# Index weights folded into the key's projection, packed sample index scores, paired value products, and projection steps placed between top-k and rotations

## The chip, the cores and the metric

The kernel runs on one core of a Trainium2 chip. The metric is the device time of one execution in microseconds (us). The kernel before took 1411.16 us, the median of three runs (1410.94 to 1413.31).

## The reference, cut to what matters

One layer of a hybrid model runs on a prompt of 512 tokens and on 8 sample sequences of 4 new tokens each (32 sample tokens), so every projection has 544 columns. The part that the change touches is the sparse attention (branch A):

```python
p = rmsnorm(x, norm_mix_g) @ w_in        # -> a_q, a_k, a_v, i_q, i_k, i_w, p_b, c_q, gates
i_q, i_k = rope_partial(...), rope_partial(...)      # 4 index heads of 64, one index key
i_w = i_w * ((4 * 64) ** -0.5)                       # one weight per token and index head
s = relu(einsum('bqhd,bld->bqhl', iq, ik))
score = einsum('bqhl,bqh->bql', s, iw)               # causal, then top-k
# prompt: 512 keys, top 128; sample: 1024 cached keys + 4 new, top 256
s = einsum(q, k_sel) * 64 ** -0.5; p = softmax(s); o = einsum(p, v_sel)   # 8 heads, 2 kv heads
```

Then follow the RWKV branch, cross attention, a gated merge, an MLP and the final norm. They are untouched.

## The kernel before, in words

Every engine has its own program, written out by hand, and semaphores order them. The projections are a list of jobs (`JOBS`). A job multiplies 8 blocks of 128 contraction rows (`KT` = 8) with the normalised input in two halves of 272 columns, 16 matmuls, all fp32; the profile has two records for each fp32 matmul. Its weights come in slabs of up to 1 MB through a ring of five (`RING`), sent by SyncE's queue (SP), which waits with a slab until the jobs of the slab five before it are done.

The stages around the change, in the order of time:

1. **First jobs.** TensorE runs four jobs (`job`, L811): `ik` (the index key, written twice, to partitions 0 to 63 and 64 to 127, by loading its weights twice), `iw` (the four index weights, 4 columns wide), and two `iq`. ScalarE evacuates each (L1453). Then three rotary rotations follow (`rope`: TensorE L864, VectorE L1782 and L1785, GpSimd L692), TensorE transposes the index weights (L884), and VectorE scales them (L1807, L1808) and copies them to the partitions of the sample's rows (L1810).
2. **Prompt top-k.** TensorE computes the prompt's index scores (L893), then the other six jobs (`aq`, `ak`, `av`). VectorE combines heads and finds the top 128 of each of three blocks of tokens with 16 rounds of `take_eight` (L1822, L1823). While it does, TensorE computes the sample's index scores (L904, L906): for each of 8 sequences a `zi` tile of 128 columns that is zero but for 16 of them, accumulated in the same banks 4 to 6.
3. **Sample scores and rotations.** VectorE applies relu and weight (L1844), TensorE sums heads with a 0/1 matrix `sel` (L911), VectorE copies the sums to `ss` (L1846, L1847). Five more rotations follow, then the transposes of the values (L921) and their copy on ScalarE (L1511, L1512).
4. **Units.** 32 units, one for each of 4 token blocks t and 8 heads (`NU` = 32; u // 8 is t). In iteration u TensorE issues the score of unit u (`p_score`, L936 and, for the mask, L938), the transposes of unit u-2 (`p_turn`, L947), the value product of unit u-3 (`p_out`, L956, output on 64 partitions) and then fill steps. VectorE in iteration u takes the maximum of unit u (L1867, L1868), normalises unit u-1 (L1873, L1874), and does one `take_eight` of the sample's top-k on `ss`. ScalarE takes the exponential (L1520) and copies the transposes (L1529). The widths grow with t: 128(t+1) keys.
5. **Sample attention** on gathered cache rows (`kvb`, from L993), then cross attention, RWKV and the rest.

**Fill steps.** `fill_plan` hands out the matmuls of later jobs (mk, mv, cq, pb, gate) one contraction block at a time to tags in TensorE's program: `fill(tag)` issues as many steps as the tag's budget says. A step is one matmul of 256 or 272 columns (L836, L839, L841). The tags ("p", u) have 5 steps each; in this stage the plan may not go past job pb 13, which leaves 160 steps (64 for mk and mv, 64 for cq, 32 for pb 12 and 13). The 160 are used up at u = 31. ScalarE evacuates a job with `evacs(tag)` where its last step was filled.

SP's queue sends, one after the other: the first slabs, 64 index-key pages (`ki`, L543), slabs 5 to 12, then the kv pages (8 groups of 8) and slabs 13 to 16.

```python
waits = [(("p", u), 5) for u in range(35)] + ...
...
for u in range(NU + 3):
    if u < NU: p_score(u)
    if 2 <= u < NU + 2: p_turn(u - 2)
    if u >= 3: p_out(u - 3)
    fill("p", u)
```

Of the kernel before, what the change touches and what calls it, by code (L numbers as in the profile page):

```python
# [27 lines left out]
P = 128  # L28
# [19 lines left out]
RING = 5  # L48
# [17 lines left out]
def constants():  # L66
# [34 lines left out]
    c["sel"][r, r % 32] = 1.0  # L101
# [30 lines left out]
def slab_plan():  # L132
# [4 lines left out]
    s = [("w_in", 0, KT, [(IK, 64), (IK, 64), (IK + 64, 4)]), ("w_in", 0, KT, [(IQ, 256)])]  # L137
# [17 lines left out]
def job_plan():  # L155


    jobs = [("ik", 0, 0, 0, 128, "a"), ("iw", 0, 0, 128, 4, "a"), ("iq", 0, 1, 0, 128, "a"), ("iq", 1, 1, 128, 128, "a")]
# [75 lines left out]
def fill_plan():  # L234
# [3 lines left out]
    waits = [(("p", u), 5) for u in range(35)] + [(("need", "cq", 3), 0), (("need", "pb", 13), 0), (("close", "p", 0), 0)]  # L238
# [42 lines left out]
KV_SLAB = slabs_before(("p",), ("need", "cq", 3), ("need", "pb", 13), ("close", "p", 0)) + RING  # L281
# [27 lines left out]
def build(nc, i, o):  # L309
    with ExitStack() as ctx:  # L310
# [84 lines left out]
        zi = R[:, B + 2048:B + 3200]  # L395
# [30 lines left out]
        iwc, iws = small[:, 0:20], small[:, 20:21]  # L426
# [364 lines left out]
        def _(pe):  # L791
# [82 lines left out]
            for n in range(4):  # L874
                job(n, xn3)
# [5 lines left out]
            out_of(1, pe)  # L881
            for t in range(5):
                w = P if t < 4 else NS
                mm = pe.transpose(ps[0:w, 7, 4 * t:4 * t + 4], iwT[0:4, P * t:P * t + w], ident[0:4, 0:4])  # L884
            mm.then_inc(s["iw_tok"], 1)

            pe.wait_ge(s["zi_set"], 5)
# [7 lines left out]
            for n in range(4, FILL0):  # L895
                job(n, xn3)

            pe.wait_ge(s["zi_set"], 4)
# [3 lines left out]
            for b in range(DB):  # L902
                for h in range(2):
                    pe.matmul(ps[:, 4 + h, :], zi[0:64, P * b:P * (b + 1)], ki[b][:, 512 * h:512 * (h + 1)],  # L904
                              start=(b == 0), stop=(b == DB - 1))
                pe.matmul(ps[:, 6, 0:NS], zi[0:64, P * b:P * (b + 1)], ik[0:64, SEQ:TOK],  # L906
                          start=(b == 0), stop=(b == DB - 1)).then_inc(s["ki_used"], 1)
            pe.wait_ge(s["rs"], 1)
            for h in range(3):
                w = 512 if h < 2 else NS  # L910
                mm = pe.matmul(ps[0:NS, 4 + h, 0:w], k_("sel"), rs[:, 512 * h:512 * h + w], start=True, stop=True)  # L911
            mm.then_inc(s["ssum"], 1)
            pe.wait_ge(s["ss_out"], 1)
            for n in range(3, 8):
                rope(n)

# [5 lines left out]
            mm.then_inc(s["v_tok"], 1)  # L922

# [8 lines left out]
            def p_score(u):  # L932
                t, ht, hp, half = unit(u)
                if u >= 3:
                    pe.wait_ge(s["p_exp"], u - 2)
# [14 lines left out]
            def p_out(u):  # L950
                t, ht, hp, half = unit(u)
                pe.wait_ge(s["p_pT_out"], u + 1)
                if u % 8 == 0 and t >= 1:
                    pe.wait_ge(s["oA_out"], t)
                for k in range(t + 1):
                    mm = pe.matmul(ps[hp, 0, P * ht:P * (ht + 1)], vt[:, k, hp], ppt[:, u % 2, k],  # L956
                                   start=(k == 0), stop=(k == t))
                mm.then_inc(s["pav_done"], 1)
# [6 lines left out]
            for u in range(NU + 3):  # L965
                if u < NU:
                    p_score(u)
                if 2 <= u < NU + 2:
                    p_turn(u - 2)
                if u == 1:  # L970
                    pe.wait_ge(s["ss_out"], 1)
                if u >= 3:
                    p_out(u - 3)
# [11 lines left out]
            quarter = [slice(32 * g, 32 * g + 32) for g in range(4)]  # L985
# [427 lines left out]
        def _(act):  # L1413
# [25 lines left out]
            def evac(n):  # L1439
# [3 lines left out]
                src = ps[0:min(w, P), b:b + 2, 0:HALF]  # L1443
                fn = ACT.Copy
# [5 lines left out]
                else:  # L1450
                    dst = {"ik": lambda: ik, "iw": lambda: iwT[0:4], "iq": lambda: iq[:, idx], "aq": lambda: aq3[:, idx],
# [48 lines left out]
            for n in range(4):  # L1500
                evac(n)
# [6 lines left out]
            for n in range(4, FILL0):  # L1508
                evac(n)
# [690 lines left out]
```

## Time and profile before

| | |
|---|---|
| median of three runs | 1411.16 us |
| the profiled execution's own time | 1411.86 us |
| its span (first to last instruction) | 1409.0 us |
| PE (TensorE matmul) busy | 1310.1 us, 93% |
| DVE (VectorE) busy | 667.4 us, 47% |
| ACT (ScalarE) busy | 370.9 us, 26% |
| chain that ended last | PE 85%, DVE 10%, ACT 2%, issue 2% |

Times are from the start of the span. A row's busy time is that of a group of instructions; a bracket behind a row is the idle time of that engine before it and what ended it. A PE record is about 0.2 us longer than the distance to the next one, because matmuls are pipelined: for a rate, subtract starts.

### The profile page before, as it was taken

To read this page: it belongs to the slowest core of one execution; us is meant where nothing else is said; L and a number is where in the kernel's file an instruction comes from. 1 tells how busy PE (TensorE), PEld (TensorE's weight loads), DVE (VectorE), ACT (ScalarE), POOL (GpSimd) and SP (SyncE) were. 2 spreads that over 40 slices of the span, in tenths; PEclk is the share of its full clock that TensorE was granted. 3 is DMA by queue.
4 is the path that set the end of the run, shared out by engine and by line. 5 is a ranking of instruction groups with operands and counts; after the bars stand their busy time and mean duration, and the time that the engine had idled before them with its cause. 6 is when DMAs were issued, how large, how long until landed. Compare 5 with 4: busy or idle time off the path is not lost.

```text
span 1409.0 us, 26535 instructions
## 1 busy us (share of the span) xinstructions
PE 1310.1 (93%) x11320; PEld 1107.2 (79%) x11324; DVE 667.4 (47%) x1119; ACT 370.9 (26%) x732; POOL 76.6 (5%) x150
## 2 busy tenths in 40 slices
PE   5898899989979999999989997989599999999995
PEld 4575566668667677688778677989599999999995
DVE  4299797744152452452343324743644334334235
ACT  3110122334323122223223222222333213223121
POOL 0100200002111021011001000000000000000000
PEclk9999899999989999999999999999899999999997
DMA  7122143404300101130220006542122222222201
GB/s 290 31 71 103 61 143 116 161 31 164 135 32 9 69 32 53 51 100 10 68 87 18 25 35 235 182 152 90 35 86 90 90 90 90 91 90 90 90 31 63
DMA packets 38646, 123.04 MB, mean 87 GB/s; under 512 B 5138, under 2 KB 17426, under 8 KB 29570
## 3 DMA queue, kind: packets, MB, share of 16 engines
q1 hardware_dynamic: 37090, 116.80, 23.6%
q0 software_dynamic: 1440, 4.56, 0.9%
q8 instruction: 89, 1.46, 0.4%
q14 instruction: 27, 0.22, 0.1%
HBM read 109.44 MB, written 11.90 MB: 86 GB/s over the span
## 4 chain that ended last, share of the span: by engine, by line
PE 85%; DVE 10%; ACT 2%; issue 2%; DMA 1%; SPq 0%; DVEq 0%; ACTq 0%
PE ps L841 23%; PE ps L1359 12%; PE ps L1360 12%; PE ps L1363 12%; PE ps L811 2%; PE ps L1110 2%; DVE R L1823 2%; DVE small L1822 2%; PE ps L936 2%; PE ps L956 2%; PE ps L836 1%; PE ps L839 1%; PE ps L1160 1%; PE ps L1196 1%; PE ps L1198 1%
## 5 line engine op out<-in xcount | busy, mean ns | idle before, releaser
L841 PE MATMUL ps<-xn,ring 128*128 128x272 f32 x1344 | 354.2, 407 | 0.9 <-ACT aq L1560 0.9
L841 PEld LDWEIGHTS ps<-xn,ring 128*128 128x128 f32 x1344 | 246.3, 192 | 61.8 <-issue 11.1
L524 DVE TENSOR_TENSOR wl<-land,wh 128x1024 fp32r<-128x1024 f32 (+1 forms) x96 | 104.7, 1092 | 193.8 <-ACT wh L516 193.0
L516 ACT ACTIVATE wh<-land 128x1024 fp32r<-128x1024 f32 (+1 forms) x96 | 91.2, 951 | 237.2 <-PE ps L1363 228.8
L1359 PE MATMUL ps<-xhi,wh 128*128 128x272 f32 x512 | 139.4, 290 | 9.0 <-DVE xlo L1775 6.8
L1360 PE MATMUL ps<-xlo,wh 128*128 128x272 f32 x512 | 139.1, 291 | 0.0
L1360 PE MATMUL ps<-hl,wh 128*128 128x272 f32 x512 | 138.2, 289 | 0.0
L1359 PE MATMUL ps<-hh,wh 128*128 128x272 f32 x512 | 138.1, 288 | 0.0
L1363 PE MATMUL ps<-xhi,wl 128*128 128x272 f32 x512 | 106.8, 290 | 0.0
L1363 PE MATMUL ps<-hh,wl 128*128 128x272 f32 x512 | 106.1, 288 | 0.0
L1359 PEld LDWEIGHTS ps<-xhi,wh 128*128 128x128 f32 x512 | 97.3, 190 | 9.9 <-issue 7.5
L1360 PEld LDWEIGHTS ps<-xlo,wh 128*128 128x128 f32 x512 | 97.4, 190 | 0.0
L1360 PEld LDWEIGHTS ps<-hl,wh 128*128 128x128 f32 x512 | 96.4, 188 | 0.0
L1359 PEld LDWEIGHTS ps<-hh,wh 128*128 128x128 f32 x512 | 96.3, 188 | 0.0
L811 PE MATMUL ps<-xn,ring 128*128 128x272 f32 (+1 forms) x320 | 76.1, 400 | 5.8 <-DVE xn L1757 3.5
L1363 PEld LDWEIGHTS ps<-xhi,wl 128*128 128x128 f32 x512 | 80.8, 190 | 0.0
L1363 PEld LDWEIGHTS ps<-hh,wl 128*128 128x128 f32 x512 | 80.1, 188 | 0.0
L811 PEld LDWEIGHTS ps<-xn,ring 128*128 128x128 f32 (+1 forms) x320 | 58.2, 183 | 24.0 <-issue 4.3
L2116 DVE TENSOR_TENSOR mlpt<-mlpt 128x544 f32<-128x544 f32 x32 | 23.2, 726 | 103.1 <-ACT mlpt L1449 103.1
L1822 DVE MAX8 small<-R 32x8 f32<-32x1056 f32 (+3 forms) x80 | 66.7, 833 | 1.6
L1823 DVE MATCH_REPLACE8 R<-small,R 32x1056 f32<-32x1056 f32 (+3 forms) x80 | 65.4, 817 | 0.0
L1449 ACT ACTIVATE mlpt<-ps 128x544 f32<-128x544 f32 x32 | 20.0, 625 | 125.5 <-PE ps L1363 125.5
(382 smaller groups left out, 2100.0 us busy)
## 6 DMA issues: line engine op xcount, KB each, us to landing
land<-in_slabs SPq DMA_DIRECT2D x36, 1024.0 KB, 4.7
ring<-in_slabs SPq DMA_DIRECT2D x29, 1024.0 KB, 5.9
gates<-R SPq DMA_DIRECT2D x24, 272.0 KB, 6.4
merge<-gates SPq DMA_DIRECT2D x24, 272.0 KB, 2.7
land<-in_slabs SPq DMA_DIRECT2D x12, 512.0 KB, 3.9
R<-in_kv SPq DMA_DIRECT2D x24, 128.0 KB, 2.0
pb<-in_kv SPq DMA_DIRECT2D x24, 128.0 KB, 2.0
xT<-in_xT SPq DMA_DIRECT2D x2, 1088.0 KB, 6.5
```

The costliest lines, as they stand in the source:

```text
L516: act.activation(hi, src, ACT.Copy).then_inc(s["weights_hi"], 1)
L524: dve.tensor_tensor(lo, src, hi.bitcast(F32), ALU.subtract).then_inc(s["weights_lo"], 1)
L811: mm = pe.matmul(ps[0:w, b + h, 0:HALF], W[:, k, c0_:c0_ + w], src[:, k, h * HALF:(h + 1) * HALF], start=(k == 0), stop=(k == KT - 1))
L841: mm = pe.matmul(ps[:, b, 0:HALF], W[:, k, c0_:c0_ + w], xn3[:, k, h * HALF:(h + 1) * HALF], start=a, stop=z)
L936: pe.matmul(ps[:, 4 + u % 3, 0:P * (t + 1)], aq3[hp, ht, P * t:P * (t + 1)], ak[hp, 0:P * (t + 1)], start=True, stop=False)
L956: mm = pe.matmul(ps[hp, 0, P * ht:P * (ht + 1)], vt[:, k, hp], ppt[:, u % 2, k], start=(k == 0), stop=(k == t))
L1110: mm = pe.matmul(ps[:, b + h, 0:HALF], w, src[:, h * HALF:(h + 1) * HALF], start=True, stop=True)
L1359: pe.matmul(ps[:, b + h, 0:HALF], whi[:, k], hi[k][:, c], start=a, stop=False)
L1360: pe.matmul(ps[:, b + h, 0:HALF], whi[:, k], lo[k][:, c], start=False, stop=False)
L1363: mm = pe.matmul(ps[:, b + h, 0:HALF], wlo[:, k], hi[k][:, c], start=False, stop=z)
L1822: step(dve.max(m8, sc))
L1823: step(dve.match_replace(sc, m8, sc, GONE))
```

## The change

- The `ik` job is 68 columns wide and holds the four index weights too; the `iw` job is gone (three jobs ahead of the rotations instead of four). ScalarE makes three copies from it: the key to partitions 0 to 63 and again to 64 to 127, and the weights.
- The sample's weights come as one column for 128 rows: VectorE builds `iwm` (4 partitions x 128), and a matmul against ones puts them in place; the separate scaling and the four small copies go.
- The sample's index scores: `zi` is 256 columns; each matmul has 32 output columns (two sequences of 16 rows), four of them side by side in the four groups of 32 partitions, two rounds. `sel` and the copies to `ss` follow the new row order; the head sums of the two halves go to partitions 0 to 31 and 32 to 63.
- New tags ("i", 0) to ("i", 7) with 28, 2, 1, 1, 1, 1, 1 and 3 steps: behind the sample's index scores, behind the head sums, behind each of the five rotations, behind the transposes of the values. The tags ("p", u) get 4 steps for u < 17 and 3 from there (4 x 17 + 3 x 18 + 38 = 160).
- `p_out` runs for two units (two heads) together, at even u from 4 on, the heads alternating within each block of keys.

```diff
-    c["sel"][r, r % 32] = 1.0
+    c["sel"][:, 0:32] = (r[:, None] // 16 == r[None, 0:32] // 4) & (r[:, None] % 4 == r[None, 0:32] % 4)
...
-    s = [("w_in", 0, KT, [(IK, 64), (IK, 64), (IK + 64, 4)]), ("w_in", 0, KT, [(IQ, 256)])]
+    s = [("w_in", 0, KT, [(IK, 64), (IK + 64, 4)]), ("w_in", 0, KT, [(IQ, 256)])]
...
-    jobs = [("ik", 0, 0, 0, 128, "a"), ("iw", 0, 0, 128, 4, "a"), ("iq", 0, 1, 0, 128, "a"), ("iq", 1, 1, 128, 128, "a")]
+    jobs = [("ik", 0, 0, 0, 68, "a"), ("iq", 0, 1, 0, 128, "a"), ("iq", 1, 1, 128, 128, "a")]
...
-    waits = [(("p", u), 5) for u in range(35)] + [(("need", "cq", 3), 0), (("need", "pb", 13), 0), (("close", "p", 0), 0)]
+    waits = [(("i", n), b) for n, b in enumerate((28, 2, 1, 1, 1, 1, 1, 3))]
+    waits += [(("p", u), 4 if u < 17 else 3) for u in range(35)] + [(("need", "cq", 3), 0), (("need", "pb", 13), 0), (("close", "p", 0), 0)]
...
-KV_SLAB = slabs_before(("p",), ("need", "cq", 3), ("need", "pb", 13), ("close", "p", 0)) + RING
+KV_SLAB = slabs_before(("i",), ("p",), ("need", "cq", 3), ("need", "pb", 13), ("close", "p", 0)) + RING
...
-        zi = R[:, B + 2048:B + 3200]
+        zi = R[:, B + 2048:B + 2304]
+        iwm = R[0:4, B + 2304:B + 2432]
...
-        iwc, iws = small[:, 0:20], small[:, 20:21]
+        iwc, iws = small[:, 0:16], small[:, 20:21]
...
-            for n in range(4):
+            for n in range(3):
                 job(n, xn3)
 
             pe.wait_ge(s["norm_rt"], 2)
             for n in range(3):
                 rope(n)
             pe.wait_ge(s["rope_sin"], 3)
-            out_of(1, pe)
-            for t in range(5):
-                w = P if t < 4 else NS
-                mm = pe.transpose(ps[0:w, 7, 4 * t:4 * t + 4], iwT[0:4, P * t:P * t + w], ident[0:4, 0:4])
-            mm.then_inc(s["iw_tok"], 1)
-
-            pe.wait_ge(s["zi_set"], 5)
+            for t in range(4):
+                pe.transpose(ps[:, 7, 4 * t:4 * t + 4], iwT[0:4, P * t:P * (t + 1)], ident[0:4, 0:4])
+            pe.wait_ge(s["zi_set"], 1)
+            pe.matmul(ps[:, 7, 16:17], iwm, k_("ones")[0:4, 0:1], start=True, stop=True).then_inc(s["iw_tok"], 1)
+
+            pe.wait_ge(s["zi_set"], 6)
             for t in range(1, 4):
...
-            for n in range(4, FILL0):
+            for n in range(3, FILL0):
                 job(n, xn3)
 
-            pe.wait_ge(s["zi_set"], 4)
             for q in range(2):
                 pe.wait_ge(s[f"ki_in{q}"], 128 * 4)
             pe.wait_ge(s["relu"], 12)
-            for b in range(DB):
-                for h in range(2):
-                    pe.matmul(ps[:, 4 + h, :], zi[0:64, P * b:P * (b + 1)], ki[b][:, 512 * h:512 * (h + 1)],
-                              start=(b == 0), stop=(b == DB - 1))
-                pe.matmul(ps[:, 6, 0:NS], zi[0:64, P * b:P * (b + 1)], ik[0:64, SEQ:TOK],
-                          start=(b == 0), stop=(b == DB - 1)).then_inc(s["ki_used"], 1)
+            quarter = [slice(32 * g, 32 * g + 32) for g in range(4)]
+            for e in range(2):
+                for h in range(3):
+                    for g in range(4):
+                        b = 2 * g + e
+                        to = 32 * b - 16 * e
+                        key = ki[b][:, 512 * h:512 * (h + 1)] if h < 2 else ik[0:64, SEQ:TOK]
+                        mm = pe.matmul(ps[quarter[g], 4 + h, 0:512 if h < 2 else NS], zi[0:64, to:to + 32], key,
+                                       start=(e == 0), stop=(e == 1))
+            mm.then_inc(s["ki_used"], 1)
+            fill("i", 0)
             pe.wait_ge(s["rs"], 1)
             for h in range(3):
                 w = 512 if h < 2 else NS
-                mm = pe.matmul(ps[0:NS, 4 + h, 0:w], k_("sel"), rs[:, 512 * h:512 * h + w], start=True, stop=True)
+                mm = pe.matmul(ps[quarter[h % 2], 4 + h, 0:w], k_("sel"), rs[:, 512 * h:512 * h + w], start=True, stop=True)
             mm.then_inc(s["ssum"], 1)
+            fill("i", 1)
             pe.wait_ge(s["ss_out"], 1)
             for n in range(3, 8):
                 rope(n)
+                fill("i", n - 1)
...
+            fill("i", 7)
...
             def p_score(u):
                 t, ht, hp, half = unit(u)
-                if u >= 3:
-                    pe.wait_ge(s["p_exp"], u - 2)
                 pe.matmul(ps[:, 4 + u % 3, 0:P * (t + 1)], aq3[hp, ht, P * t:P * (t + 1)], ak[hp, 0:P * (t + 1)],
...
             def p_out(u):
-                t, ht, hp, half = unit(u)
-                pe.wait_ge(s["p_pT_out"], u + 1)
+                t, ht = unit(u)[:2]
+                pe.wait_ge(s["p_pT_out"], u + 2)
                 if u % 8 == 0 and t >= 1:
                     pe.wait_ge(s["oA_out"], t)
                 for k in range(t + 1):
-                    mm = pe.matmul(ps[hp, 0, P * ht:P * (ht + 1)], vt[:, k, hp], ppt[:, u % 2, k],
-                                   start=(k == 0), stop=(k == t))
-                mm.then_inc(s["pav_done"], 1)
+                    for m in range(2):
+                        hp = unit(u + m)[2]
+                        mm = pe.matmul(ps[hp, 0, P * ht:P * (ht + 1)], vt[:, k, hp], ppt[:, (u + m) % 2, k],
+                                       start=(k == 0), stop=(k == t))
+                mm.then_inc(s["pav_done"], 2)
...
             for u in range(NU + 3):
                 if u < NU:
+                    if u >= 3:
+                        pe.wait_ge(s["p_exp"], u - 2)
                     p_score(u)
                 if 2 <= u < NU + 2:
                     p_turn(u - 2)
-                if u == 1:
-                    pe.wait_ge(s["ss_out"], 1)
-                if u >= 3:
-                    p_out(u - 3)
+                if u >= 4 and u % 2 == 0:
+                    p_out(u - 4)
                 fill("p", u)
...
+                if kind == "ik":
+                    act.activation(h2(ik[0:64]), src[0:64], ACT.Copy)
+                    act.activation(h2(ik[64:128]), src[0:64], ACT.Copy)
+                    act.activation(h2(iwT[0:4]), src[64:68], ACT.Copy).then_inc(s["evac_a"], 1)
+                    return
...
-            for n in range(4, FILL0):
+            for n in range(3, FILL0):
                 evac(n)
+            act.wait_ge(s["ki_used"], 1)
+            for n in range(7):
+                evacs("i", n)
...
+            evacs("i", 7)
...
+            out_of(job_at("ik"), dve)
+            dve.tensor_tensor(iwm.rearrange("p (b h q) -> p b h q", b=DB, h=4),
+                              iwT[0:4, SEQ:TOK].rearrange("p (b q) -> p b q", q=4).unsqueeze(2).to_broadcast([4, DB, 4, 4]),
+                              ident[0:4, 0:4].unsqueeze(1).unsqueeze(3).to_broadcast([4, DB, 4, 4]),
+                              ALU.mult).then_inc(s["zi_set"], 1)
...
-                dst = zi[0:64, 32 * h:32 * h + DB * 132].rearrange("p (b c) -> p b c", c=132)[:, :, 0:4]
+                dst = zi[0:64].rearrange("p (b c) -> p b c", b=DB)[:, :, 4 * h:4 * h + 4]
                 dve.tensor_copy(dst, iq[hp, h // 2, SEQ:TOK].rearrange("p (b q) -> p b q", q=4)).then_inc(s["zi_set"], 1)
 
             dve.wait_ge(s["iw_tok"], 1)
-            step(dve.tensor_scalar(iwc[:, 0:16], ps[:, 7, 0:16], 0.0625, None, ALU.mult))
-            step(dve.tensor_scalar(iwc[0:NS, 16:20], ps[0:NS, 7, 16:20], 0.0625, None, ALU.mult))
-            for h in range(4):
-                ins = dve.tensor_copy(iws[32 * h:32 * h + 32], iwc[0:NS, 16 + h:17 + h])
-                if h < 3:
-                    step(ins)
-                else:
-                    ins.then_inc(s["zi_set"], 1)
-            dve.wait_ge(s["zi_set"], 5)
+            step(dve.tensor_scalar(iwc, ps[:, 7, 0:16], 0.0625, None, ALU.mult))
+            dve.tensor_scalar(iws, ps[:, 7, 16:17], 0.0625, None, ALU.mult).then_inc(s["zi_set"], 1)
+            dve.wait_ge(s["zi_set"], 6)
             flat = ps[:, 4:7].rearrange("p a b -> p (a b)")[:, 0:KEYS]
...
-            dve.wait_ge(s["ki_used"], 8)
+            dve.wait_ge(s["ki_used"], 1)
             dve.tensor_scalar(rs, flat, 0.0, iws, ALU.max, ALU.mult).then_inc(s["rs"], 1)
             dve.wait_ge(s["ssum"], 1)
-            step(dve.tensor_copy(ss[:, 0:PAST], flat[0:NS, 0:PAST]))
+            for h in range(2):
+                step(dve.tensor_copy(ss[:, 512 * h:512 * (h + 1)], ps[32 * h:32 * h + 32, 4 + h, :]))
             dve.tensor_tensor(ss[:, PAST:KEYS], flat[0:NS, PAST:KEYS], k_("snew")[0:NS], ALU.add).then_inc(s["ss_out"], 1)
```

## Rows read from the trace of the kernel before

**Rows 1.** ScalarE in order of time (start us, us): evacuation of the fourth job.
```profile
59.94 0.62 ACT L1453 ACTIVATE R<-ps 128x544 f32<-128x544 f32 x1 [6.71 <-PE ps L811]
```

**Rows 2.** VectorE: start of the prompt's top-k and what follows its end.
```profile
69.58 0.35 DVE L1832 TENSOR_SCALAR R<-R,small 128x256 f32<-128x256 f32 x1 [1.47 <-ACT R L1507]
...
139.64 1.32 DVE L1844 TENSOR_SCALAR R<-ps,small 128x1056 f32<-128x1056 f32 x1
...
144.78 1.21 DVE L1846 COPY R<-ps 32x1024 f32<-32x1024 f32 x1 [3.82 <-PE ps L911]
```

**Rows 3.** TensorE: sample index scores (first, last) and the head sums.
```profile
121.58 1.98 PE L904 MATMUL ps<-R 64*128 64x512 f32 x4
...
136.98 0.30 PE L906 MATMUL ps<-R 64*128 64x32 f32 x2
141.01 3.73 PE L911 MATMUL ps<-R,cst 128*32 128x512 f32 x6 [3.73 <-DVE R L1844]
```

**Rows 4.** Stretches: start:end, length, engines' busy us (records), granted clock, DMA share, GB/s.
```profile
139.00:141.00 2.00, 0.00 (x0) 0.00 (x0) 1.89 (x3) 0.00 (x0) 0.00 (x0) 0.50 0.00 0
...
158.00:159.00 1.00, 0.56 (x2) 0.50 (x2) 0.00 (x0) 0.98 (x3) 1.00 (x2) 0.50 0.31 33
```

**Rows 5.** A long stretch; engines PE, PEld, DVE, ACT, POOL.
```profile
164.00:292.00 128.00, 127.37 (x584) 85.65 (x587) 106.56 (x210) 35.90 (x112) 1.07 (x2) 1.00 0.38 124
```

**Rows 6.** VectorE: the maximum that begins iteration u, for u = 1, 5, 6, 15, 31.
```profile
163.74 0.29 DVE L1867 TENSOR_REDUCE small<-ps 128x1 f32<-128x128 f32 x1 [1.29 <-PE ps L938]
...
177.36 0.29 DVE L1867 TENSOR_REDUCE small<-ps 128x1 f32<-128x128 f32 x1
...
180.76 0.29 DVE L1867 TENSOR_REDUCE small<-ps 128x1 f32<-128x128 f32 x1
...
214.09 0.42 DVE L1867 TENSOR_REDUCE small<-ps 128x1 f32<-128x256 f32 x1 [0.56 <-DVE R L1823]
...
292.02 0.69 DVE L1867 TENSOR_REDUCE small<-ps 128x1 f32<-128x512 f32 x1 [1.34 <-issue]
```

**Rows 7.** TensorE: one iteration at t = 3 and the start of the next.
```profile
285.16 1.12 PE L936 MATMUL ps<-R,aq 64*128 64x512 f32 x2
...
286.97 1.09 PE L956 MATMUL ps<-R 128*64 128x128 f32 x8
287.99 2.56 PE L841 MATMUL ps<-xn,ring 128*128 128x272 f32 x10
290.48 1.12 PE L936 MATMUL ps<-R,aq 64*128 64x512 f32 x2
```

**Rows 8.** VectorE in order of time: the index weights.
```profile
66.99 0.15 DVE L1808 TENSOR_SCALAR small<-ps 32x4 f32<-32x4 f32 x1
67.18 0.68 DVE L1810 COPY small<-small 32x1 f32<-32x1 f32 x4
```

**Rows 9.** TensorE: four products of 32 output columns side by side.
```profile
300.89 0.62 PE L993 MATMUL ps<-xT,R 128*32 128x512 f32 x2 [1.21 <-ACT aq L1534]
300.91 0.62 PE L993 MATMUL ps<-R 128*32 128x512 f32 x2
301.32 0.62 PE L993 MATMUL ps<-xT,R 128*32 128x512 f32 x2
```

**Rows 10.** SP's queue: slabs 5 to 12, then the first 16 kv pages.
```profile
99.90 92.69 SPq L593 DMA_DIRECT2D ring<-in_slabs  x8
193.37 18.53 SPq L543 DMA_DIRECT2D xT<-in_kv  x16
```

**Rows 11.** TensorE: one of the five later rotations.
```profile
152.06 1.15 PE L864 MATMUL ps<-R,cst 128*128 128x272 f32 x4 [0.91 <-DVE R L1782]
```

**Rows 12.** TensorE: the last value products (units 30 and 31).
```profile
297.84 1.85 PE L956 MATMUL ps<-R 128*64 128x128 f32 x16
```

**Rows 13.** ScalarE: the evacuation of the second half of a pb job.
```profile
295.90 0.37 ACT L1485 ACTIVATE pb<-ps 128x240 f32<-128x240 f32 x1 [1.71 <-PE ps L841]
296.17 0.19 ACT L1486 ACTIVATE pb<-ps 128x32 f32<-128x32 f32 x1
```

More of the change, by code:

```diff
@@ L984, in _ @@
             pe.wait_ge(s["oA_out"], 4)
-            quarter = [slice(32 * g, 32 * g + 32) for g in range(4)]
             for hb in range(2):
@@ L1450, in evac @@
                 else:
-                    dst = {"ik": lambda: ik, "iw": lambda: iwT[0:4], "iq": lambda: iq[:, idx], "aq": lambda: aq3[:, idx],
+                    dst = {"iq": lambda: iq[:, idx], "aq": lambda: aq3[:, idx],
                            "ak": lambda: ak, "av": lambda: av}[kind]()
@@ L1499, in _ @@
             act.wait_ge(s["norm_out"], 16)
-            for n in range(4):
+            for n in range(3):
                 evac(n)
```

## Prediction

> **What bounds the kernel now.** I read the engine table first: TensorE is busy 93% of the span, so the question for each stage is whether TensorE or something else ends last in it. The chain of waits says VectorE carries 10%, and nearly all of its top-k lines lie ahead of 300 us, where the change is. So I cut that part into stages and read each in order of time.
>
> First jobs: TensorE alone. The fourth job's evacuation stands 6.71 + 0.62 = 7.33 us behind the third's [rows 1], 16 steps of 0.458 us.
>
> Prompt top-k: VectorE alone, from 69.58 to 139.64 us, with no wait that matters; TensorE finishes the sample's index scores at 137.3 and then sits idle [rows 2, 3]. What is taken from TensorE here gives nothing by itself.
>
> Sample scores and rotations: a relay of small pieces. VectorE and TensorE wait for each other, and the granted clock is at the low level (0.50, 1.2 GHz) after the idle time [rows 4].
>
> Units, 164 to 292 us: TensorE busy 127.37 of 128 us, VectorE 106.56 [rows 5]. TensorE is the bound, and VectorE waits for its score: not at all at t = 0 (iterations follow at 180.76 - 177.36 = 3.40 us with no idle time), 0.56 us at t = 1, 1.34 us at t = 3 [rows 6]. An iteration at t = 3 takes 5.32 us [rows 7]. So VectorE needs 3.40 us at t = 0 and 5.32 - 1.34 = 3.98 at t = 3; its widths grow evenly, so I take 3.59 and 3.79 between.
>
> **The change part by part.**
>
> *The iw job goes.* It is one of four jobs ahead of the first rotation, -7.33 us [rows 1], whole, since rotations, scores and top-k hang behind it. The key's third copy on ScalarE (0.62 us each [rows 1]) ends about 2 us behind job 0, while TensorE works 7.3 us on job 1; its bank is needed only by job 2. The new VectorE product for the weights falls into VectorE's idle time before the rotations. If that cover were gone it would cost one small operation, 0.2 us. The slab of job 1 is wanted 7.3 us earlier, at about 37 us, and was issued at 4.
>
> *Index weights.* The scaling at 66.99 stays as one instruction (0.15 us); the four copies of 0.68 us go [rows 8]. TensorE's scores and so the top-k start 0.7 us earlier still. The small matmul takes the place of a transpose. Sum so far: -8.0 us. The top-k then runs its 70.06 us [rows 2] unchanged and ends at 131.6.
>
> *Sample index scores.* Before: 121.58 to 137.3, 15.7 us [rows 3]. Four products of 32 columns side by side start a set of 512 columns every 0.86 us: records of two different tile pairs begin at 300.89 and 300.91, the next at 301.32 [rows 9]. Two rounds of (0.86 + 0.86 + 0.13) with two changes of tile shape are 3.9 us. Those rows have 128 contraction rows, these have 64; the bound on the other side is no overlap, 15.7 us. I take 3.9: it is the same column split. Worth nothing directly, for VectorE hides it; it makes the room for the first 28 fill steps. TensorE gets there at 121.6 - 8.0 = 113.6, has the scores at 117.5, and the 28 steps (256 of 272 columns: 0.43 us each, 0.2 us for the group) end at 129.8, before 131.6 + 1.3 (the relu). So the 28 steps are free with 3 us to spare. Their slabs, 5 and 6, leave SP at 99.9 us [rows 10]; that does not move earlier, since 64 page loads stand ahead, but it is 17 us before use.
>
> The Trainium skill ("TensorE: Matmul & The Clock Gate", Part 3, The mechanism) speaks against this part: a weight load overlaps with a matmul under way only when its row group differs, and here all four column groups share their rows. By its load figure (columns / 1.2 GHz) an estimate is 27 ns for each of 96 records, 1.3 us on the hidden scores. The same rule would put some 53 ns on each of 160 value-product records. The products of 32 columns [rows 9] share their rows as well and leave no gap for a load, so the trace disagrees and I charge nothing.
>
> *Head sums.* Before 141.01 to 144.78 = 3.77 us at the low clock [rows 2, 3, 4]. TensorE will again have been idle for 3 us, so I assume the low clock; the two 512-column sums run side by side: 3.77 less two records of 0.85 = 2.1 us, -1.6 us. Bounds: 3.8 (no overlap), 1.2 (overlap and full clock). The copy of 1.21 us is split in two, +0.2 us for the second start. The two fill steps lie beside these copies.
>
> *Fill steps between rotations.* A later rotation comes every 0.91 + 1.15 = 2.06 us, of which TensorE is idle 0.91 us while VectorE works [rows 11], so one step of 0.43 to 0.65 us fits: 0 to 3.3 us for the five, I take +0.2 (the second rotation is just late). *Three steps behind the value transposes* stand ahead of unit 0's score, while ScalarE copies the values for 1 us: 1.5 us at full clock, 2.8 at the low one, which the stage had at 158 us [rows 4]. Part of it returns, since iteration 0 has one step fewer and was itself held by the low clock (VectorE waited 1.29 us at u = 1 [rows 6]). I take +0.4 at u = 1; bounds -1.0 to +2.0. Sum up to u = 1: -8.0 - 1.6 + 0.2 + 0.2 + 0.4 = -8.8 us.
>
> *Units.* The fill steps go from 5 to 4 and then 3: -0.46 and -0.92 us per unit. The value product of 1.02 us at t = 3 [rows 7] serves two units. New TensorE time at t = 3: 5.32 - 0.92 - 0.51 = 3.89 us on average, at t = 0: 3.4 - 0.43 - 0.18 = 2.8. VectorE's 3.98 and 3.40 are above both, so VectorE becomes the bound everywhere, barely at t = 3. Even iterations are heavier there (4.4 against 3.4 us). But a score may start as soon as the exponential two units back is done, and a transpose needs only the normalisation early in VectorE's previous iteration, so TensorE can stand 1 to 2 us ahead and 0.5 us of unevenness is absorbed. ScalarE's copy of an even unit now waits for the pair's product in the same iteration, and behind it the next exponential; VectorE needs that only one whole iteration later. From u = 1 to 31: 7 x 3.40 + 8 x 3.59 + 8 x 3.79 + 7 x 3.98 = 110.7 us, against 292.02 - 163.74 = 128.3 [rows 6]. That is -17.6 us.
>
> *The end of the units.* Before, from VectorE's u = 31 (292.02) to the first sample product (300.89) 8.9 us [rows 6, 9]; the last two value products ran alone (297.84, 1.7 us [rows 12]). Now, counted from the same point: the last transpose ends at 5.6, three fill steps 7.2, the pair 8.2, three steps 9.8, ScalarE's two copies of the pb half (0.56 us [rows 13]) and the signal 10.6, which the sample product waits for. +1.7 us; bounds 0 to +3.
>
> *The queue.* Slabs 10 to 12 wait for mk and mv jobs, which end up to 35 us earlier, so the kv pages start near 160 us instead of 193.37; 16 of them took 18.5 us [rows 10], 64 take 74, and they are in by 235, the sample attention wants them at 276. Nothing is exposed. All fill steps of the stage are used in both kernels, so behind it the work is the same and only shifts.
>
> Sum: -8.8 - 17.6 + 1.7 = -24.7 us. The profiled execution took 1411.86, which gives 1387.2; it stood 0.7 above the median of the runs, so I predict 1386.5 us.
>
> **Rivals.**
>
> *Sample scores do not overlap with 64 contraction rows.* For it: no row of this form. Scores end at 129.3, the 28 steps at 141.6, and the head sums wait 8.6 us for TensorE behind them, less 1 for a warm clock. 1394 us. A lost front gain of another kind (a slab or a page late) lands in the same place.
>
> *TensorE stays the bound in the units*, because value products of different heads run one after the other (then t = 3 takes 4.40 instead of 3.98, 8 x 0.4 = 3.4 us) or more fill groups cost more: 1390 to 1392. Against: the overlap of [rows 9].
>
> *VectorE is the bound already*, its idle time only the shape of the relay. Then the units give nothing and -8.8 + 1.7 is left: 1404 us. Against: idle time that grows with TensorE's widths [rows 6].
>
> *Slower: the clock falls in the units.* TensorE will wait 0.6 us in each 3.4 at t = 0. If that brought the granted clock to 0.50, a unit would cost TensorE about 2 x 3.5 = 7.0 instead of 3.7 us, +3.3. From 24.7 / 3.3, some 8 of 32 units on, the kernel is slower than before; with half of them it takes 1386.5 + 53 = 1439 us. Against: it would be fully busy at once at the low clock and so recover, as it did between 158 and 164 us.
>
> **How the numbers follow.** Forecast 0.68 (own range 1383.5 to 1389.5), TensorE bound 0.11, late sample scores 0.09, units give nothing 0.06, slower 0.04, that front and units together change nothing 0.02. Range 1382.5 to 1396: it holds the first three and the unknown terms. What this measurement can tell from no change is about 0.2%, 2.8 us; only the last two cases fall inside or beyond it. Faster 0.94, same 0.02, slower 0.04.
>
> **What would show it.** The fourth evacuation (now aq) falls behind the first rotations, and the top-k starts at 61.5 and ends at 131.6. The sample scores take 3.9 us and the fills behind them end before the relu. VectorE's maxima in the units show no idle time before them and distances of 3.4 to 4.0 us, TensorE small gaps with the clock at 1.00. The pair's product takes about 1 us for two heads at t = 3. I am wrong if VectorE still waits for scores at t = 3, if TensorE's fills run past the relu, or if the head sums or unit 0 start later than this shift.

## The result and the profile after

The changed kernel took 1387.41 us (median of four runs, 1384.62 to 1390.13), the kernel before 1412.08 (four runs): a ratio of 0.982, 95% interval 0.9806 to 0.9834, or 24.7 us less. Measured a second time, the changed kernel gave 0.9796 (0.9779 to 0.9813).

The profiled execution of the changed kernel took 1390.13 us with a span of 1388.4 us, the longest of its four. Distances are therefore compared stage by stage. Each row gives the start of the same event in both profiles; the last column is what that stage alone added to the shift. "First sample product" is the first matmul of the sample attention. "First weight slab behind the gates" is the first slab that SP's queue sends once all jobs up to the gates are done; what stands behind it is the same work in every kernel here.

| event | before | after | moved by | that stage alone |
|---|---|---|---|---|
| first rotation on VectorE | 60.85 | 54.97 | -5.88 | -5.88 |
| prompt top-k starts | 69.58 | 62.58 | -7.00 | -1.12 |
| relu and weights of the sample scores | 139.64 | 132.62 | -7.02 | 0.0 |
| copy of the head sums | 144.78 | 135.13 | -9.65 | -2.63 |
| first of the five rotations | 147.53 | 138.08 | -9.45 | +0.20 |
| maximum of unit 0 | 159.46 | 150.94 | -8.52 | +0.93 |
| maximum of unit 1 | 163.74 | 153.95 | -9.79 | -1.27 |
| maximum of unit 31 | 292.02 | 264.92 | -27.10 | -17.31 |
| first sample product | 300.89 | 274.85 | -26.04 | +1.06 |
| first weight slab behind the gates | 852.28 | 827.44 | -24.84 | +1.20 |
| end of the span | 1409.0 | 1388.4 | -20.6 | +4.2 |

VectorE in the changed kernel (start, us, engine, line, operation). The first three rows answer to [rows 2]; the others are maxima of u = 0, 1, 8, 9, 16, 17, 30 and 31, for [rows 6]:

```profile
62.58 0.35 DVE L1847 TENSOR_SCALAR R<-R,small 128x256 f32<-128x256 f32 x1 [1.05 <-ACT R L1519]
...
132.62 1.32 DVE L1859 TENSOR_SCALAR R<-ps,small 128x1056 f32<-128x1056 f32 x1
135.13 1.40 DVE L1862 COPY R<-ps 32x512 f32<-32x512 f32 x2 [1.20 <-PE ps L916]
...
150.94 0.29 DVE L1883 TENSOR_REDUCE small<-ps 128x1 f32<-128x128 f32 x1 [2.65 <-PE ps L944]
153.95 0.29 DVE L1883 TENSOR_REDUCE small<-ps 128x1 f32<-128x128 f32 x1
...
177.79 0.42 DVE L1883 TENSOR_REDUCE small<-ps 128x1 f32<-128x256 f32 x1
181.33 0.42 DVE L1883 TENSOR_REDUCE small<-ps 128x1 f32<-128x256 f32 x1
...
206.57 0.56 DVE L1883 TENSOR_REDUCE small<-ps 128x1 f32<-128x384 f32 x1
210.31 0.56 DVE L1883 TENSOR_REDUCE small<-ps 128x1 f32<-128x384 f32 x1
...
260.92 0.69 DVE L1883 TENSOR_REDUCE small<-ps 128x1 f32<-128x512 f32 x1
264.92 0.69 DVE L1883 TENSOR_REDUCE small<-ps 128x1 f32<-128x512 f32 x1
```

No maximum from u = 1 to 31 has a bracket, and no other VectorE row of that stretch has one: VectorE never waits. Its distances are 3.40, 3.60, 3.80 and 4.00 us at t = 0 to 3.

TensorE in the changed kernel, for [rows 3], [rows 7] and the three steps ahead of unit 0:

```profile
116.25 0.62 PE L909 MATMUL ps<-R 64*32 64x512 f32 x2
...
119.94 12.35 PE L838 MATMUL ps<-pb,ring 128*128 128x256 f32 x56
133.99 1.11 PE L916 MATMUL ps<-R,cst 128*32 128x512 f32 x6 [1.70 <-DVE R L1859]
...
147.33 2.76 PE L841 MATMUL ps<-ring,pb 128*128 128x256 f32 x6
150.03 0.71 PE L942 MATMUL ps<-R,aq 64*128 64x128 f32 x2
...
250.43 0.66 PE L953 MATMUL ps<-cst,R 128*128 128x128 f32 x4 [0.40 <-DVE R L1890]
251.13 1.09 PE L964 MATMUL ps<-R 128*64 128x128 f32 x16
252.16 1.18 PE L843 MATMUL ps<-xn,ring 128*128 128x272 f32 x4
```

All 24 sample score matmuls take 119.94 - 116.25 = 3.7 us, with 64 contraction rows. The 28 steps end at 132.3, 0.3 us before VectorE's relu starts and 1.7 us before the head sums, where the prediction had 3 us to spare: TensorE reached the scores at 116.25 instead of 113.6. Its last four jobs ahead of them took 31.2 us, 29.5 before, and the granted clock was 0.50 at 86 to 88 us, behind a wait of 2.68 us. From the start of the head sums to the copy it is 1.14 us. A pair's 16 records take 1.03 us at t = 3, as one unit's 8 did, and TensorE now waits for VectorE's normalisation.

Stretches of the changed kernel (columns as in [rows 4]): before the head sums, before unit 0, and the units:

```profile
132.00:134.00 2.00, 0.30 (x4) 0.01 (x2) 1.87 (x3) 0.00 (x0) 0.00 (x0) 1.00 0.00 0
148.00:150.00 2.00, 2.00 (x5) 1.09 (x4) 0.25 (x2) 1.60 (x3) 1.60 (x3) 0.50 0.46 35
154.00:265.00 111.00, 102.49 (x502) 63.34 (x503) 106.85 (x211) 32.81 (x106) 1.06 (x2) 1.00 0.39 124
```

VectorE is busy 106.85 of 111 us in the units, TensorE 102.49. In [rows 5] it was 106.56 and 127.37 of 128.

### The profile page after: what moved, and what is told of

Its sections match the earlier page's. It is cut to its first block, busy times and chain, and to the rows that moved or that the text cites. A ratio compares the mean times of both kernels' runs of the same rounds, so it can differ in the third digit from the quotient of the medians.

```text
span 1388.4 us, 26471 instructions
## 1 busy us (share of the span) xinstructions
PE 1285.1 (93%) x11290; PEld 1091.2 (79%) x11293; DVE 667.1 (48%) x1117; ACT 370.5 (27%) x733; POOL 75.7 (5%) x150
## 4 chain that ended last, share of the span: by engine, by line
PE 76%; DVE 18%; DMA 2%; ACT 2%; issue 1%; SPq 0%; DVEq 0%; ACTq 0%
PE ps L843 20%; PE ps L1366 12%; PE ps L1367 12%; PE ps L1370 12%; DVE R L1838 5%; DVE small L1837 5%; PE ps L1117 2%; PE ps L813 2%; DVE small L1883 1%; PE ps L1167 1%; PE ps L1203 1%; DMA merge<-gates 1%; DVE R L1890 1%; PE ps L1205 1%; PE ps L1180 1%
## 5 line engine op out<-in xcount | busy, mean ns | idle before, releaser
L813 PE MATMUL ps<-xn,ring 128*128 128x272 f32 (+1 forms) x288 | 71.0, 411 | 6.8 <-DVE xn L1773 4.2
L813 PEld LDWEIGHTS ps<-xn,ring 128*128 128x128 f32 (+1 forms) x288 | 55.1, 192 | 23.0 <-issue 6.2
```

Source lines behind the costliest of these rows:

```text
L813: mm = pe.matmul(ps[0:w, b + h, 0:HALF], W[:, k, c0_:c0_ + w], src[:, k, h * HALF:(h + 1) * HALF], start=(k == 0), stop=(k == KT - 1))
```

## Experiments

Marks named below are the ones of the table; "units" is the distance between the maxima of u = 1 and 31, "end" the distance from the maximum of u = 31 to the first sample product. The changed kernel has units 110.97 and end 9.93.

### Old budgets, products paired

```diff
-    waits = [(("i", n), b) for n, b in enumerate((28, 2, 1, 1, 1, 1, 1, 3))]
-    waits += [(("p", u), 4 if u < 17 else 3) for u in range(35)]
+    waits = [(("i", n), b) for n, b in enumerate((0,) * 8)]
+    waits += [(("p", u), 5) for u in range(35)]
```

> The changed kernel with the fill budgets of before: none in the i tags, 5 in each unit; value products stay paired. My theory (with 5 steps TensorE is the bound again from t = 1 on, and pairs take 0.3 to 0.5 us off a unit): VectorE's maxima u = 1 to 31 span about 121 us (changed kernel 111.0, before 128.3), with idle time before them at t = 2 and 3; the end of the units is about 1.5 us shorter than in the changed kernel; total about 1396.5 us. Rival (pairing is worth nothing): the span is 128 and the total about 1404. Rival (the moved steps are worth nothing, the pairs did it): span 111, total within 1 us of the changed kernel.

Measured: 1394.64 us, ratio 0.9866 (0.9849 to 0.9883). Units 117.62, end 8.40. VectorE's maxima at the end of the stage:

```profile
256.89 0.69 DVE L1883 TENSOR_REDUCE small<-ps 128x1 f32<-128x512 f32 x1
262.21 0.69 DVE L1883 TENSOR_REDUCE small<-ps 128x1 f32<-128x512 f32 x1 [1.35 <-issue]
266.32 0.69 DVE L1883 TENSOR_REDUCE small<-ps 128x1 f32<-128x512 f32 x1
271.64 0.69 DVE L1883 TENSOR_REDUCE small<-ps 128x1 f32<-128x512 f32 x1 [1.35 <-issue]
```

TensorE is the bound again, in every second iteration, the one behind a pair. But VectorE first waits at u = 21, where the sum I made puts TensorE behind from t = 1 on: it had a lead to use up (from 184 to 236 us TensorE is busy without a break, and VectorE still does not wait until u = 21). So pairs alone, with the old budgets, take 10.7 of the 17.3 us, more than the 7 to 8 that I gave them, and the price of undoing the steps is 6.7 us in the units.

The steps also did something ahead of the units. Without the 28 of them TensorE stood idle for 13.98 us and the granted clock was 0.50 when the head sums came:

```profile
132.45 2.02 PE L916 MATMUL ps<-R,cst 128*32 128x512 f32 x6 [13.98 <-DVE R L1859]
```

They took 2.06 us to the copy (134.51) instead of 1.14, and from the relu to the first of the five rotations it was 7.37 us instead of 5.46. At u = 1, 1.6 us of that was left.

### Products one at a time

```diff
-                if u >= 4 and u % 2 == 0:
-                    p_out(u - 4)
+                if u >= 3:
+                    p_out(u - 3)
```

(with the body of `p_out` as before)

> The changed kernel with one value product per unit at iteration u - 3, as before; budgets as changed. My theory (VectorE is the bound, TensorE passes it only at t = 3, 4.40 against 3.98 us): maxima u = 1 to 31 span about 114 us, +3 us, all of it at t = 3; total 1390.5 us. Rival (pairs carry half of the gain in the units): span about 120, total 1396. Rival (VectorE hides them fully): no change.

Measured: 1389.34 us, ratio 0.9834 (0.9818 to 0.9851). Units 111.87, end 12.12. TensorE at the end of the stage:

```profile
272.87 1.09 PE L962 MATMUL ps<-R 128*64 128x128 f32 x8
273.89 1.64 PE L843 MATMUL ps<-xn,ring 128*128 128x272 f32 x6
276.08 0.62 PE L998 MATMUL ps<-xT,R 128*32 128x512 f32 x2 [0.55 <-ACT pb L1496]
```

The 3 us that I expected are there (0.9 + 2.2), most of them not where I looked: TensorE lives on its lead until u = 28. Behind the last maximum, 1.24 us of the 2.2 come because it reaches the next transposes later, and 0.95 because three products follow them instead of two pairs. The steps alone take 16.4 of the 17.3 us in the units, the pairs alone 10.7. The two are not parts of a sum. Both take work from the same bound, until VectorE is it.

### Sample scores, one column group after the other

```diff
-            for e in range(2):
-                for h in range(3):
-                    for g in range(4):
+            for g in range(4):
+                for e in range(2):
+                    for h in range(3):
```

> The changed kernel with the same 24 sample score matmuls, but all six of one column group in a row, so that neighbours in the queue use the same columns. My theory (neighbours in different column groups run side by side, these don't): scores take about 14.3 us instead of 3.7, the 28 fill steps behind them end at about 143 us, the head sums start there instead of at 134.0; total +9 us, 1396 us. Rival (TensorE overlaps groups whatever the order): scores stay near 4 us, no change. Rival (top-k hides the scores, so their speed never mattered): scores 14.3 us, total unchanged.

Measured: 1391.88 us, ratio 0.9848 (0.9832 to 0.9865), 4.5 us more than the changed kernel and half of the 9 expected. TensorE:

```profile
116.24 5.92 PE L909 MATMUL ps<-R 64*32 64x512 f32 x21
...
127.91 12.35 PE L838 MATMUL ps<-pb,ring 128*128 128x256 f32 x56
140.20 1.11 PE L916 MATMUL ps<-R,cst 128*32 128x512 f32 x6
```

The same matmuls take 11.7 us instead of 3.7 (14.3 expected), so it is the order in the queue that lets them overlap. They are not serial altogether: at each change of group a few records of neighbours lie side by side. The head sums start 6.2 us later, the first sample product 5.7. The score's own speed is hidden; what shows is the end of the 28 steps behind it against VectorE's relu at 133.9.

### Sixteen matmuls more ahead of the rotations

```diff
+            out_of(1, pe)
+            for k in range(KT):
+                for h in range(2):
+                    pe.matmul(ps[:, 2 + h, 0:HALF], ident, xn3[:, k, h * HALF:(h + 1) * HALF], ...)
```

> The changed kernel with 16 more matmuls of 128 x 272 ahead of the first rotation, in the place of the iw job that went; their result is not used. My theory (everything behind hangs on TensorE here): the top-k starts 7.33 us later, at about 69.9 us, and all behind it shifts by the same; total 1394.7 us. Rival (part of it is hidden behind VectorE or a load): less than 5 us.

Measured: 1392.13 us (1388.04 to 1393.49), ratio 0.9844 (0.9823 to 0.9864). The evacuation of job 1 and the first rotation's product on VectorE:

```profile
47.13 0.62 ACT L1470 ACTIVATE R<-ps 128x544 f32<-128x544 f32 x1 [5.40 <-PE ps L813]
...
62.71 0.72 DVE L1803 TENSOR_TENSOR R<-ps,cst 128x544 f32<-128x544 f32 x1 [20.67 <-PE ps L866]
```

Between them 15.58 us; in the changed kernel 54.97 - 46.72 = 8.25. The difference is 7.33 us, the term of the sum. It reaches the first sample product (282.79, +7.9), and the median of the whole shows +4.7, which its runs, 5.5 us apart, do not separate from 7.3. Part of the difference lies behind the gates: that stretch took 557.4 us in this profile and 561.0 in the changed kernel's (see the last experiment).

### More work on VectorE, in both kernels

```diff
+                if u < NU:
+                    step(dve.max(small[0:NS, 72:80], ss[:, 0:512]))
```

> The changed kernel with one more maximum over 512 columns on VectorE in each of the 32 units (about 0.72 us, result not used). My theory (VectorE is the bound in every unit): maxima u = 1 to 31 span 111.0 + 30 x 0.72 = about 132.6 us, total about 1410 us. Rival (TensorE is still the bound at t = 2 and 3): under 15 us more.

> The kernel before with the same extra maximum in each unit. My theory (VectorE is the bound only up to about u = 12, then its idle time takes it up): maxima u = 1 to 31 span 128.3 + about 9.5 = 138 us, total about 1421.5 us. Rival (VectorE was the bound already): +22 us.

Measured: on the changed kernel 1409.86 us, ratio 0.9973 (0.9962 to 0.9984), units 132.48 (+21.5), no maximum from u = 1 on that waits. On the kernel before 1419.87, ratio 1.0049 (1.0034 to 1.0064), units 134.87 (+6.6). In the kernel before with the load, the maxima of u = 27 and 28, the first that waits since u = 1:

```profile
280.07 0.69 DVE L1867 TENSOR_REDUCE small<-ps 128x1 f32<-128x512 f32 x1
285.37 0.69 DVE L1867 TENSOR_REDUCE small<-ps 128x1 f32<-128x512 f32 x1 [0.62 <-PE ps L938]
```

This shows the bound directly. The same operation costs 0.72 us in each unit of the changed kernel and is hidden, but for a third, in the kernel before. There VectorE is then the bound up to u = 27 and TensorE's lead does the rest, so even less than the 9.5 us that I expected comes through.

The changed kernel with the load also shows the rival of the falling clock at work. TensorE is busy 115.88 of 133 us there, and its granted clock falls again and again, first here:

```profile
156.00:160.00 4.00, 2.51 (x10) 2.00 (x11) 3.83 (x9) 0.90 (x4) 0.00 (x0) 0.86 0.91 324
160.00:164.00 4.00, 3.92 (x13) 2.13 (x13) 3.83 (x9) 0.63 (x3) 0.00 (x0) 0.50 0.47 143
```

Later stretches of 4 us have 0.65 (at 180 us), 0.57 (196), 0.50 (224), 0.60 (240) and 0.57 (268). Each time TensorE is then almost fully busy, the clock comes back within a few us, and no maximum of VectorE waits: the units cost what the extra work costs, and nothing for the clock. Only the end is longer, 11.50 us.

### Steps moved away from the path

```diff
+    waits = [(("i", n), b) for n, b in enumerate((31, 2, 1, 1, 1, 1, 5, 0))]
+    waits += [(("p", u), 4 if u == 0 else 5 if u < 7 else 4 if u < 16 else 3 if u < 32 else 0) ...]
```

and, by itself, only `(31, 2, 1, 1, 1, 1, 1, 0)`.

> The changed kernel with the same 160 fill steps at other places: i tags 31, 2, 1, 1, 1, 1, 5, 0; units 4 at u = 0, 5 for u = 1 to 6, 4 for u = 7 to 15, 3 for u = 16 to 31, none at u = 32 to 34. My theory (the three steps ahead of unit 0 and the nine behind the last unit stand on the path, the others don't): unit 0's maximum 1.5 to 2 us earlier, the span of u = 1 to 31 unchanged at 111, and from the last maximum to the first sample product 8.9 instead of 9.9 us; total about -3 us, 1384.4 us. Rival (the steps cost the same wherever they stand): no change.

> The changed kernel with only the three steps behind the value transposes moved to the first i tag (31 and 0); units as in the changed kernel. My theory: unit 0's maximum about 1.3 us earlier, the rest as it was; total -1.3 us, 1386.1 us. Rival (TensorE then goes cold and loses it again in the first units): unchanged at u = 1.

Measured: moved steps 1383.6 us, ratio 0.9787 (0.9773 to 0.98); i7 alone 1386.55, ratio 0.9816 (0.9803 to 0.983). Moved steps: units 110.96, end 8.79. From the start of the top-k to the maxima of u = 0 and 1: changed kernel 88.36 and 91.37 us, i7 alone 87.01 and 91.54, moved steps 86.51 and 89.52. TensorE in the i7 kernel, then its stretch, then the stretch in the kernel with moved steps:

```profile
146.90 0.76 PE L942 MATMUL ps<-R,aq 64*128 64x128 f32 x2 [1.04 <-ACT R L1527]
...
147.67 3.73 PE L841 MATMUL ps<-ring,pb 128*128 128x256 f32 x8
```

```profile
148.00:150.00 2.00, 2.00 (x6) 1.55 (x6) 1.93 (x5) 0.73 (x3) 0.00 (x0) 0.50 0.69 228
```

```profile
148.00:150.00 2.00, 1.96 (x10) 1.72 (x11) 1.27 (x3) 1.54 (x3) 1.22 (x3) 1.00 0.72 53
```

Taking the three steps away gives 1.35 us at unit 0, and the low clock takes it back in the four steps of unit 0 (3.7 us instead of 1.9): at u = 1 nothing is left. The rival was right there. Five steps in TensorE's idle time behind the last rotation keep the clock at 1.00, and then the gain stays: 1.85 us at u = 1. The end is 1.14 us shorter as expected. Counted from the start of the top-k, the trace has the first sample product 3.0 us earlier than in the changed kernel, and the first slab behind the gates 3.7 us (761.14 against 764.86). In the medians it is 3.8 us against the first measurement of the changed kernel and 1.4 against the second, whose interval overlaps this one.

### All steps early

```diff
+    waits += [(("p", u), 5) for u in range(35)]
```

(i tags as changed)

> The changed kernel with its i tags, but 5 steps in each unit until the 122 left are used up (u = 0 to 24) instead of 4 and 3. My theory (TensorE may run about 4 us ahead of VectorE; 5 steps put it behind by 0.24 us a unit at t = 1 and 0.53 at t = 2, 6 us in all): maxima u = 1 to 31 span about 113 us (changed 111.0), idle time before them only at u = 19 to 25, and 8.4 instead of 9.9 us from the last maximum to the first sample product; total about 1388 us. Rival (only the number of steps moved out of the units counts, not their spread): span 111 and total 1386. Rival (no lead, each late unit counts): span 117.

Measured: units 112.76 with idle time of VectorE only at u = 21, 23 and 24, near the expected 113; but end 9.74, not 8.4. TensorE has no steps from u = 25 on, is busy 3.78 of 7 us behind 260, and its clock falls, to a mean of 0.75 from 252 to 260 us and to 0.50 behind 267:

```profile
260.00:267.00 7.00, 3.78 (x27) 2.08 (x27) 6.79 (x12) 2.07 (x6) 0.00 (x0) 0.95 0.00 0
267.00:277.00 10.00, 6.74 (x44) 4.80 (x48) 4.85 (x10) 3.06 (x6) 0.00 (x0) 0.50 0.01 2
```

The last pair takes 1.98 us instead of 1.03. The profiled execution took 1389.55 us; two more stood at 1393.43 and 1393.8 (a fourth took 7066.96 us and is left out), ratio 0.9861 (0.9841 to 0.9882), where 1388 was expected. Why those two are 4 us above the profiled one stays open; the profiled one had the short stretch behind the gates (557.9 us, see the last experiment), which the long one would have made some 3 us longer.

### The last round of top-k later

```diff
-                for _ in range(TOPK_S // 8 * u // NU, ...):
+                if u != NU - 1:
                     take_eight(ss, m8[0:NS])
```

(on top of the moved steps; the 32nd round then runs behind the normalisation of unit 31)

> The kernel with moved steps (31, 2, 1, 1, 1, 1, 5, 0 and none behind the last unit), and VectorE's round of top-k of unit 31 moved behind the normalisation of unit 31. My theory (VectorE is the bound up to the last normalisation, and its mask is wanted only by the sample attention): from the last maximum to the first sample product about 7.1 instead of 8.8 us, the rest unchanged; total 1.7 us less than with moved steps, 1382 us. Rival (the mask is then late): no change.

Measured: 1382.22 us, ratio 0.9769 (0.975 to 0.9788). The lowest median here, but its interval overlaps that of the moved steps, so the 1.4 us between them are not shown. In the trace the end is 6.91 us, 1.88 less. VectorE:

```profile
263.24 0.69 DVE L1883 TENSOR_REDUCE small<-ps 128x1 f32<-128x512 f32 x1
...
265.16 0.49 DVE L1890 TENSOR_SCALAR R<-R,small 128x512 f32<-128x512 f32 x1
265.57 1.24 DVE L1837 MAX8 small<-R 32x8 f32<-32x1056 f32 x1
...
268.18 0.70 DVE L1896 TENSOR_SCALAR R<-R 32x1056 bf16<-32x1056 f32 x1
```

The mask is done at 268.9, ahead of the first sample product at 270.15. So the mask is not late. But the gain does not last. Counted from the start of the top-k, the first sample product comes 1.87 us earlier than with the moved steps, and the first slab behind the gates at 761.16 us, where the moved steps have 761.14. In the stretch from 280 to 284 us the granted clock is 0.58 here and 1.00 there, and nine transposes behind the sample scores take 2.18 us instead of 1.20. That explains about one microsecond of the loss; where the rest goes was not looked for.

### Both kernels once more

> The changed kernel itself once more, on this chip. The stretch from the first weight slab behind the gates to the end took 561.0 us in the changed kernel's profile and 556.7 in the profile before, with the same work. If that is scatter of one execution, it may come out at either here; if the change causes it, it is 561 again.

> The kernel before itself once more: the same question for the stretch behind the gates, 556.7 us in its first profile. Scatter: either value. Caused by the change: 556.7.

Measured: changed 1385.04 us; before 1412.57 (one run). From the first slab behind the gates to the end: changed 560.3 us (561.0 the first time), before 557.6 (556.7). Over all profiles the code behind the gates, which is the same everywhere, took 556.5 to 557.9 us in seven and 560.0 to 561.0 in seven: the kernel before and its variant short all three times, the changed kernel long twice, its variants four short and five long. So the changes to the part ahead do not fix it, and it is not settled whether they make the long case likelier.

## Why the prediction was right, step by step

**Iw job and index weights.** Predicted -7.33 and -0.7. The extra matmuls measured the first at 7.33 us, and the second is 1.12 in the profile. At the first rotation the profile shows only -5.88. The first job itself began 0.9 us later in this execution and the jobs ended 1.45 later than the sum says. This looks like scatter of the start: in the three profiles with four jobs the first rotation stands at 60.85, 61.94 and 63.14 us; in the ten with three jobs it stands at 53.2 to 53.5 in four, 7.3 to 7.7 below the 60.85, and at 54.4 to 55.3 in six.

**Sample scores.** 3.7 us against 3.9, overlap with 64 contraction rows as with 128. The rule of the Trainium skill ("TensorE: Matmul & The Clock Gate", Part 3, The mechanism), that a weight load overlaps only where the row group differs, would have left gaps; the records follow each other at 0.43 us as in [rows 9], so it does not bind here. (The prediction's 27 ns for each of 96 records is 2.6 us and not 1.3; the 24 matmuls have 48 records, which gives its 1.3. The sum does not use it.)

**Head sums.** Mis-sized: 1.14 us to the copy against 2.1. I assumed the low clock after 3 us of idle time. TensorE was idle for only 1.7 us, since the 28 steps ended 2.5 us later than I had put them, and the clock stayed at 1.00. It earned 1 us more. Where the clock was low, with the old budgets, the same matmuls took 2.06 us: the size was right for the low clock, the clock was not. Ending later was a gain here, since it left less idle time ahead of the head sums.

**Between the copy and u = 1.** The split copy was predicted at +0.2 and measured +0.20. Behind it +0.6 was predicted and 0.93 - 1.27 = -0.34 measured. The steps between the rotations are hidden: on VectorE the five rotations take 9.25 us in both kernels. The three behind the transposes ran at the low clock and cost 1.35 us at unit 0, as the run without them shows (0.93 is what is left of it against the kernel before), but they are what brought the clock back by unit 1.

**Units.** -17.6 predicted, -17.3 measured: VectorE became the bound in every unit, with 3.40 to 4.00 us as read from its idle time before. The load experiments show it. What failed is what I then expected of each part alone, 121 and 114 us: either alone does better, 117.62 and 111.87, because TensorE's lead carries it through much of the stage.

**End of the units.** +1.7 predicted, +1.06 measured. The order of events is the predicted one; the last transposes began 4.75 us behind the last maximum and were done some 0.3 us earlier than I had it, and the two copies on ScalarE added 0.5 us instead of 0.8. Without the steps behind the last unit the end is 1.14 us shorter, so they are the cause.

**Rivals.** The sample scores overlap. Issued in a row, at 11.7 us, they would have cost 5.7 to 6.2 us; with no overlap at all they were not measured. The clock did not fall in the units of the changed kernel (1.00), though TensorE waited. It did fall inside the units in two others, where VectorE had more work and where the steps ran out at u = 25, and in the first of them it cost nothing, for the reason that the prediction gave against this rival: at the low clock TensorE is almost fully busy at once, and the clock comes back. The forecast of a rise of 3.3 us for each unit at the low clock was never put to the test.

**How good the total is.** 24.7 us were predicted for the profile and 24.7 lie between the medians, which is partly luck. At the first sample product the trace has -26.04: 1.0 us less than predicted ahead of the top-k, 1.0 more at the head sums, 0.9 more up to u = 1, 0.3 less in the units, 0.6 more at the end. Behind it 5.4 us are lost again, of which 4.2 are the scatter behind the gates. The kv pages were sent from 157.73 to 230 us, about as predicted, and the first sample product waited for ScalarE and not for them.

## What to carry to other kernels

Read the idle time of the second-busiest engine inside a stage: it is the most that any relief of the first can bring (17.3 us here), and two reliefs share it. Filler work on TensorE is best put where another engine holds the path, and it does two things there: it takes work out of a bound stage, and it keeps the clock up for the short matmuls behind it. Put matmuls of different column groups next to each other in the queue. And follow a gain past its own stage: the last round of top-k gave 1.88 us that were gone further on.

## What the runs showed of the hardware

- The granted clock rewards filler work. Without the three steps ahead of unit 0 it was 0.50 in the four that followed; with five steps earlier it stayed at 1.00. TensorE busy 102 of 111 us kept 1.00; busy 116 of 133 us it fell to 0.50 to 0.65 in six stretches of 4 us; busy 3.78 of 7 us it had 0.95, and then 0.50 for 10 us.
- What the low clock costs depends on who waits for TensorE: nothing in the units with the extra load, 0.9 us at the head sums (2.06 against 1.14).
- For products of 32 columns with 64 contraction rows the order in the queue alone is worth a factor of three (11.7 against 3.7 us).
- The same code behind the gates takes 556.5 to 561.0 us from one execution to the next; this alone is 0.3% of the kernel. None of the fourteen profiles lies between 557.9 and 560.0.
